# The product that picks the tokens of the second expert pair, moved ahead of the first pair's gate and up products

## The chip, the cores and the metric

The kernel runs on one NeuronCore of a Trainium2 chip. The metric is the device time of one execution in microseconds (us). Three executions of the kernel before took 1514.11, 1519.95 and 1521.13 us; their median is 1519.95 us. A fourth execution was recorded by the hardware profiler and took 1516.05 us. All rows shown here come from that one. In the profile, PE is TensorE (the matrix engine), PEld its weight loads, DVE is VectorE, ACT is ScalarE, POOL is GpSimd and SP is SyncE, the engine that issues the large DMAs. An issue on a queue of an engine is written SPq, ACTq or POOLq.

## The reference

One step of a hybrid decoder with one layer: 256 prompt tokens and 8 sample tokens, width 2048. After the attention part (stick-breaking and forgetting heads, a paged cache, an output projection, a residual add) comes a mixture of 32 experts, of which each token uses two. The part that matters here is this, cut from the reference:

```python
u = rms_norm(h, norm_ffn_g)                       # 264 tokens x 2048
lg = u @ w_rg + b_rg                              # choice of 1 of 4 groups
le = einsum('td,gde->tge', u, w_re) + b_re        # choice of 2 of 8 experts in it
comb = one_hot(chosen experts) * gate             # 264 x 32
h = silu(u @ w_gate[e]) * (u @ w_up[e])           # per expert e, 2048 -> 256
f = sum_e (h * comb[:, e]) @ w_down[e]            # 256 -> 2048
y = rms_norm(h_residual + f, norm_final_g)
```

Everything is float32. The weights of an expert are three matrices of 2 MB each, so the 32 experts are 96 loads of 2048 KB.

## The kernel before, in words

The kernel computes expert by expert, two experts (a pair, k = 0 and 1) at a time, in 16 pairs numbered n. A pair has 128 slots for tokens, 64 for each expert; the first 8 slots of each expert hold the 8 sample tokens, the others prompt tokens that were routed to it. There may be further pairs for experts that overflow; they are guarded by a run-time test.

Each pair needs these steps, and the engines take them in a fixed order that the program text sets:

- **tokens(n)** on PE (L1901): 32 matrix products of 128x128 with a 0/1 selection `pick_tok`, made by POOL, that pick the prompt tokens of pair n out of `qo` and leave them transposed in banks 4 to 7 of the accumulator memory. ACT copies the four banks to `xgT` (`tokens` on ACT, L2012), but not before the gate and up products of the pair before have read the old `xgT` (semaphore gu1).
- **gate_up(k, n)** on PE (L1912 and L1914): gate and up product of expert k. It waits for its two weights in the buffer `ws`, slots 3k and 3k+1.
- **turn_over(k, n)** on PE (L1921): two transposes of the result, after DVE has copied it to `gu`.
- **silu** on ACT (L2020) and a multiplication on DVE (L2120) give `hT`.
- **down(k, n)** on PE (L1934): the down product, with the weight in slot 3k+2; it waits for `hT`. In all pairs with a following pair the whole of `xgT` for that next pair has to be written first: `pe.wait_ge(E["xgT"], 4 * n + 8)` stands ahead of down(0, n), since down writes banks 4 to 7.
- POOL scatters the result rows to memory (`y_rows`).

The order on PE in a pair is gate_up(0), gate_up(1), turn_over(0), tokens(n+1), turn_over(1), down(0), down(1). On ACT it is silu(0), tokens(n+1), silu(1), and a copy of half the down result.

Pair 0 is special. Its tokens were picked at the end of the attention part (L1148). The sample tokens are finished only here: PE sums their rows in `sample_rows` (L1941, 32 products with 8 columns as the profile counts them) between the two gate_up, DVE normalises them, PE computes their router logits in `sample_logits` (L1949) behind gate_up(1), and DVE runs `sample_route`, a chain of some 25 small operations that ends in `s_r` (L2094, semaphore sr2). ACT waits for sr2, computes one exponential (L2045), and only then enters its own pair 0: silu(0), tokens(1), silu(1). On PE, turn_over(1, 0) waits for slc 3, the two additions that take the logits out of bank 3.

SP loads the weights. There are six slots, one for each weight of a pair, so a load of pair n+1 can only be issued once the product of pair n that reads the slot has finished. The order of issue is slots 0, 1 (waiting for gate_up(0)), 3, 4 (gate_up(1)), 2 (down(0)), 5 (down(1)), see L170. The six weights of pair 0 are issued earlier, as the output projection frees the slots.

Of the kernel before, what the change touches and what calls it, by code (L numbers as in the profile page):

```python
# [75 lines left out]
def wait_past(eng, sem, value):  # L76

    if not isinstance(value, int) or value > 0:
        eng.wait_ge(sem, value)
# [642 lines left out]
def token_cols(qo, t, c):  # L722

    return qo[:, 8 * t + c // 2, c % 2 * P:(c % 2 + 1) * P]
# [1025 lines left out]
def experts(nc, ctx, ws, W, a, ident, ones, iota, gcol, lastq, xT, xn, qo, xgT, in_slot, in_pair, pick_tmp, pick_tok, wr, br, bank, sem, E, dest, gates, extra,  # L1750
# [48 lines left out]
    with nc.Block() as block:  # L1799
# [91 lines left out]
        def _(pe):  # L1891
            def tokens(n, stored, i):


                pe.wait_ge(E["xg"], n + 1)
                wait_past(pe, E["yc0"], 2 * stored)
                wait_past(pe, E["yc1"], 2 * stored)
                for k in range(4):
                    for c in range(4):
                        for t in range(2):  # L1900
                            mm = pe.matmul(bank[4 + k][:, c * P:(c + 1) * P], token_cols(qo, t, 4 * k + c), pick_tok[:, i, t, :],  # L1901
                                           start=(t == 0), stop=(t == 1))
                    mm.then_inc(E["xgp"], 1)

            def gate_up(k, n):

                wg, wu = 3 * k, 3 * k + 1
                pe.wait_ge(W[wg], 16 * (n + FIRST[wg]))
                pe.wait_ge(W[wu], 16 * (n + FIRST[wu]))
                for c in range(KC):  # L1910
                    lhs = xgT[:, c, k * SLOTS:(k + 1) * SLOTS]
                    pe.matmul(bank[2 * k][0:SLOTS, 0:256], lhs, ws[:, wg, c * 256:(c + 1) * 256],  # L1912
                              start=(c == 0), stop=(c == KC - 1))
                    mm = pe.matmul(bank[2 * k][SLOTS:P, 0:256], lhs, ws[:, wu, c * 256:(c + 1) * 256],  # L1914
                                   start=(c == 0), stop=(c == KC - 1))
                mm.then_inc(E[f"gu{k}"], 1)

            def turn_over(k, n):
                pe.wait_ge(E[f"guc{k}"], n + 1)
                for j in range(2):  # L1920
                    mm = pe.transpose(bank[2 * k + 1][:, j * P:(j + 1) * P], gu[k][:, :].rearrange("s (p j) -> s j p", j=2)[:, j, :],  # L1921
                                  ident[:, :])
                mm.then_inc(E[f"t{k}"], 1)

            def down(k, n):

                wd = 3 * k + 2
                pe.wait_ge(W[wd], 16 * (n + FIRST[wd]))
                pe.wait_ge(E[f"h{k}"], n + 1)
                for dc in range(2):  # L1930
                    for j in range(2):
                        for q in range(4):
                            h0, d0 = q // 2 * HALF, j * D + q % 2 * 1024 + dc * 512
                            mm = pe.matmul(bank[4 + 2 * k + dc][q * HALF:(q + 1) * HALF, :], hT[k][:, j, h0:h0 + HALF],  # L1934
                                           ws[:, wd, d0:d0 + 512], start=(j == 0), stop=(j == 1))
                mm.then_inc(E[f"y{k}"], 1)

            def sample_rows():
                part = xn[:, :, :].rearrange("p c t -> p (c t)")
                for c in range(KC):  # L1940
                    mm = pe.matmul(bank[3][:, c * NB:(c + 1) * NB], part[:, c * P:(c + 1) * P], lastq[:, 0:NB], start=True, stop=True)  # L1941
                mm.then_inc(E["sf"], 1)

            def sample_logits():

                pe.wait_ge(E["sun"], 1)
                for c in range(KC):
                    for r0 in (0, HALF):
                        mm = pe.matmul(bank[3][r0:r0 + NB, P:P + NG + NE], xn[:, c, SEQ:T], wr[:, c, 0:NG + NE],  # L1949
                                       start=(c == 0), stop=(c == KC - 1))  # L1950
                mm.then_inc(E["sl"], 1)

            def sample_rest():

                pe.wait_ge(E["yc0"], 2 * EXP_PAIRS - 2)
                pe.wait_ge(E["dst"], 1)
                pe.wait_ge(F["sel"], 1)
                pe.transpose(bank[4][:, 0:P], x_s[:, :, :].rearrange("p n c -> p (n c)"), ident[:, :])
                pe.matmul(bank[4][:, P:P + 2], spread[:, :], gates[0:NB, 2, :], start=True, stop=True).then_inc(F["hs"], 1)

            def pair(n, ahead, first=False, last=False, i=0):
                pe.wait_ge(E["xgT"], 4 * n + 4)
                gate_up(0, n)
                if last:
                    sample_rest()
                if first:
                    sample_rows()
                gate_up(1, n)
                if first:
                    sample_logits()  # L1970
                turn_over(0, n)
                if ahead:
                    tokens(n + 1, n, i)
                if first:
                    pe.wait_ge(E["slc"], 3)
                turn_over(1, n)
                if ahead:
                    pe.wait_ge(E["xgT"], 4 * n + 8)
                if last:
                    pe.wait_ge(F["hsc"], 2)  # L1980
                down(0, n)
                down(1, n)

            pair(0, True, True, i=1)
            with pe.Fori(0, EXP_PAIRS // 2 - 1) as m:
                for i in range(2):
                    pair(2 * m + 1 + i, True, i=i)
            pair(EXP_PAIRS - 1, False, last=True)
            with pe.If(in_use(pe, 0) > 0):
                for n in range(EXP_PAIRS, PAIRS):  # L1990
# [219 lines left out]
```

## Time and profile before

| what | value |
|---|---|
| median of three runs | 1519.95 us |
| profiled execution | 1516.05 us |
| span of its instructions | 1514.3 us |
| PE busy, of the span | 1315.7 us (87%) |
| DVE busy | 673.4 us (44%) |
| ACT busy | 233.6 us (15%) |
| read from memory over the span | 558.26 MB, 379 GB/s with the writes |

The 1.75 us between the span and the time of the execution lie outside the first and last instruction. Busy shares are averages over the attention part (to about 991 us) and the expert part (from there on), which have different limits; the stage that the change touches has to be read by itself. A stretch is given as "from:to" in us from the start of the span. The DMA share of a stretch is the mean busy share of the 16 DMA engines, and it can read slightly above 1. PEclk is the clock granted to TensorE, where 1.00 is 2.4 GHz and 0.50 is 1.2 GHz.

### The profile page before, as it was taken

To read this page: it belongs to the slowest core of one execution; us is meant where nothing else is said; L and a number is where in the kernel's file an instruction comes from. 1 tells how busy PE (TensorE), PEld (TensorE's weight loads), DVE (VectorE), ACT (ScalarE), POOL (GpSimd) and SP (SyncE) were. 2 spreads that over 40 slices of the span, in tenths; PEclk is the share of its full clock that TensorE was granted. 3 is DMA by queue.
4 is the path that set the end of the run, shared out by engine and by line. 5 is a ranking of instruction groups with operands and counts; after the bars stand their busy time and mean duration, and the time that the engine had idled before them with its cause. 6 is when DMAs were issued, how large, how long until landed. Compare 5 with 4: busy or idle time off the path is not lost. (4 is left out here: it accounts for less than half of the span.)

```text
span 1514.3 us, 26133 instructions
## 1 busy us (share of the span) xinstructions
PE 1315.7 (87%) x8622; PEld 870.3 (57%) x8622; DVE 673.4 (44%) x4778; ACT 233.6 (15%) x453; POOL 75.4 (5%) x119
## 2 busy tenths in 40 slices
PE   7999788889789899856899987789999999999992
PEld 4678455566556566533667743466666565655561
DVE  4437855676676675677846466021000100000004
ACT  2111002112212212213011021101111010111011
POOL 1000000000000000001000001001100010001000
PEclk8899989899999999976999998979999999999997
DMA  9776999999999999999999989999999999999984
GB/s 302 248 260 229 385 397 391 396 383 381 382 377 390 383 379 392 387 405 398 351 403 402 401 320 390 399 414 379 422 428 428 427 424 423 422 419 414 416 341 178
DMA packets 170382, 570.39 MB, mean 377 GB/s; under 512 B 17401, under 2 KB 75562, under 8 KB 156954
## 3 DMA queue, kind: packets, MB, share of 16 engines
q1 hardware_dynamic: 145616, 541.70, 91.4%
q10 hardware_dynamic: 21762, 22.58, 4.3%
q0 software_dynamic: 2896, 4.86, 0.9%
q8 instruction: 45, 0.74, 0.2%
q14 instruction: 63, 0.52, 0.1%
HBM read 558.26 MB, written 15.67 MB: 379 GB/s over the span
## 5 line engine op out<-in xcount | busy, mean ns | idle before, releaser
L128 DVE CUSTOM_DVE_ANT_0 ws<-ws,xgT 128x128 f32<-128x128 f32 x1792 | 387.8, 284 | 204.7 <-DMA ws<-in_cache_fox_k 186.0
L979 PE MATMUL bank<-xn,ws 128*128 128x264 f32 x1152 | 289.9, 407 | 10.5 <-DMA ws<-in_w_in 10.5
L979 PEld LDWEIGHTS bank<-xn,ws 128*128 128x128 f32 x1152 | 223.0, 199 | 110.9 <-issue 54.8
L1912 PE MATMUL bank<-ws,xgT 128*64 128x256 f32 x1024 | 231.4, 386 | 16.7 <-DMA ws<-in_w_expert_up 12.1
L1914 PE MATMUL bank<-ws,xgT 128*64 128x256 f32 x1024 | 231.5, 386 | 0.0
L964 PE MATMUL bank<-ws,PR 128*32 128x512 f32 x1024 | 150.8, 668 | 78.3 <-DMA ws<-in_cache_fox_v 73.8
L1912 PEld LDWEIGHTS bank<-ws,xgT 128*64 128x64 f32 x1024 | 140.3, 139 | 104.6 <-issue 22.2
L128 DVE DVE_READ_ACCUMULATOR2_ANT Z<- 128x1 f32 x1792 | 141.8, 79 | 0.0
L1914 PEld LDWEIGHTS bank<-ws,xgT 128*64 128x64 f32 x1024 | 140.3, 139 | 0.0
L2113 DVE COPY gu<-bank 128x256 f32<-128x256 f32 x32 | 13.6, 425 | 269.4 <-PE bank L1914 269.4
L1084 PE MATMUL bank<-qo,ws 128*128 128x256 f32 x512 | 117.0, 387 | 6.2 <-DVE qo L1521 5.2
L1934 PE MATMUL bank<-ws,hT 128*32 128x512 f32 x1024 | 113.2, 594 | 7.1 <-ACT xgT L2012 6.9
L1084 PEld LDWEIGHTS bank<-qo,ws 128*128 128x128 f32 x512 | 97.7, 193 | 31.5 <-issue 16.6
L1901 PE MATMUL bank<-xg,qo 128*128 128x128 f32 x960 | 109.7, 275 | 0.0
L1901 PEld LDWEIGHTS bank<-xg,qo 128*128 128x128 f32 x960 | 108.5, 192 | 0.0
L964 PEld LDWEIGHTS bank<-ws,PR 128*32 128x32 f32 x1024 | 21.5, 112 | 119.8 <-DMA ws<-in_cache_fox_v 91.8
L523 PE MATMUL bank<-xn,ws 128*128 128x264 f32 x384 | 86.8, 387 | 0.0
L523 PEld LDWEIGHTS bank<-xn,ws 128*128 128x128 f32 x384 | 72.6, 190 | 14.1 <-issue 2.0
L1934 PEld LDWEIGHTS bank<-ws,hT 128*32 128x32 f32 x1024 | 32.0, 110 | 76.7 <-issue 67.0
L607 DVE CUSTOM_DVE_ANT_0 ws<-ws,xgT 128x128 f32<-128x128 f32 x256 | 55.3, 287 | 39.5 <-DMA ws<-in_cache_sb_k 15.6
L2120 DVE TENSOR_TENSOR hT<-si,bank 128x128 f32<-128x128 f32 x32 | 9.2, 288 | 108.3 <-ACT si L2020 108.2
L1848 POOL DMA_INDIRECT y_rows<-ys,dest x32 | 29.5, 922 | 403.6 <-DVE ys L2124 338.6
(433 smaller groups left out, 971.4 us busy)
## 6 DMA issues: line engine op xcount, KB each, us to landing
ws<-in_cache_sb_k SPq DMA_DIRECT2D x128, 512.0 KB, 9.1
ws<-in_cache_fox_k SPq DMA_DIRECT2D x128, 512.0 KB, 13.0
ws<-in_cache_sb_v SPq DMA_DIRECT2D x128, 512.0 KB, 9.2
ws<-in_cache_fox_v SPq DMA_DIRECT2D x128, 512.0 KB, 12.8
ws<-in_w_expert_gate SPq DMA_DIRECT2D x32, 2048.0 KB, 16.1
ws<-in_w_expert_up SPq DMA_DIRECT2D x32, 2048.0 KB, 20.0
ws<-in_w_expert_down SPq DMA_DIRECT2D x32, 2048.0 KB, 16.9
ws<-in_w_in SPq DMA_DIRECT2D x24, 2048.0 KB, 21.3
```

The costliest lines, as they stand in the source:

```text
L128: ins = dve.tensor_tensor_reduce(k, k, qb[:, (g * H + h) * HD:(g * H + h + 1) * HD], 1.0, 0.0, ALU.mult, ALU.add, Z[:, n % 2, g, h, t:t + 1])
L523: mm = pe.matmul(bank[4 + k % 4][:, 0:T], chunk(n)[:, c, m * P:(m + 1) * P], xn[:, c, :], start=(c == 0), stop=(c == KC - 1))
L607: ins = dve.tensor_tensor_reduce(k, k, qb[:, (g * H + h) * HD:(g * H + h + 1) * HD], 1.0, 0.0, ALU.mult, ALU.add, Z[:, 0, g, h, t:t + 1])
L964: mm = pe.matmul(bank[0][r0:r0 + 32, :], PR[:, g, t, :], vring[:, u, g, half * 512:(half + 1) * 512], start=(t == 0), stop=(t == PAGES - 1))
L979: mm = pe.matmul(out[:, 0:T], w[:, c, m * P:(m + 1) * P], xn[:, c, :], start=(c == 0), stop=(c == KC - 1))
L1084: mm = pe.matmul(out, ws[:, 4 + r, k0:k0 + P], qo[:, 8 * r + c, 0:SEQ], start=(r == 0 and c == 0 and m % 2 == 0), stop=(r == 1 and c == 7) ...
L1848: pool.indirect_dma_start(y_half, bass.IndirectOffsetOnAxis(ap=dest[0:rows, 2 * n + k:2 * n + k + 1], axis=0), ys[k][0:rows, :], None, bou ...
L1901: mm = pe.matmul(bank[4 + k][:, c * P:(c + 1) * P], token_cols(qo, t, 4 * k + c), pick_tok[:, i, t, :], start=(t == 0), stop=(t == 1))
L1912: pe.matmul(bank[2 * k][0:SLOTS, 0:256], lhs, ws[:, wg, c * 256:(c + 1) * 256], start=(c == 0), stop=(c == KC - 1))
L1914: mm = pe.matmul(bank[2 * k][SLOTS:P, 0:256], lhs, ws[:, wu, c * 256:(c + 1) * 256], start=(c == 0), stop=(c == KC - 1))
L1934: mm = pe.matmul(bank[4 + 2 * k + dc][q * HALF:(q + 1) * HALF, :], hT[k][:, j, h0:h0 + HALF], ws[:, wd, d0:d0 + 512], start=(j == 0), stop ...
L2113: dve.tensor_copy(gu[k][:, :], bank[2 * k][:, 0:256]).then_inc(E[f"guc{k}"], 1)
```

## The change

For pair 0 alone, the call of tokens(1) is taken from its place between turn_over(0, 0) and turn_over(1, 0) and put ahead of gate_up(0, 0). The other pairs keep their order. Nothing is added or taken away, and no other engine's program is changed: ACT still copies the picked tokens behind silu(0), and not before gu1.

```diff
             def pair(n, ahead, first=False, last=False, i=0):
                 pe.wait_ge(E["xgT"], 4 * n + 4)
+                if first:
+                    tokens(n + 1, n, i)
                 gate_up(0, n)
                 if last:
                     sample_rest()
@@
                 if first:
                     sample_logits()
                 turn_over(0, n)
-                if ahead:
+                if ahead and not first:
                     tokens(n + 1, n, i)
                 if first:
                     pe.wait_ge(E["slc"], 3)
```

The first place is on PE at the start of the expert part. L1746 and L1890 are branches at the block's entry, L1901 is tokens, L1912 and L1914 are the gate and the up product. A row "x32" is 32 instructions of the program in a row.

```order
 L1746 UNCONDITIONAL_BRANCH
 L1890 UNCONDITIONAL_BRANCH
+L1901 MATMUL bank<-xg,qo 128x128 x32
 L1912 MATMUL bank<-ws,xgT 64x256
 L1914 MATMUL bank<-ws,xgT 64x256
```

The 32 products of tokens(1) now stand ahead of the first gate product.

The second place is on PE behind gate_up(1, 0). L1949 is sample_logits, L1921 the transposes of turn_over, L1934 the down products.

```order
 L1914 MATMUL bank<-ws,xgT 64x256
 L1949 MATMUL bank<-wr,xn 8x36 x32
-L1921 MATMUL bank<-ident,gu 128x128 x2
-L1901 MATMUL bank<-xg,qo 128x128 x32
-L1921 MATMUL bank<-ident,gu 128x128 x2
+L1921 MATMUL bank<-ident,gu 128x128 x4
 L1934 MATMUL bank<-ws,hT 32x512 x32
```

Nothing but the four transposes is left between the logits and the down products.

## Rows read from the trace of the kernel before

**Rows 1.** Page, part 4: the chain that ended last, by line.
```profile
DMA ws<-in_w_expert_up 14%; PE bank L1912 11%; PE bank L1934 3%; PE bank L1901 2%; PE bank L1914 0%; DVE ws L2138 0%; DMA ws<-y_rows 0%; ACT xgT L2012 0%; SPq L170 0%; PE bank L1941 0%; DVE ws L2155 0%; DMA y_rows<-ys,dest 0%; DVE ws L2144 
```

**Rows 2.** Stretches: PE, PEld, DVE, ACT, POOL busy, PEclk, DMA share, GB/s.
```profile
1028.00:1030.00 2.00, 2.00 (x24) 0.64 (x20) 0.05 (x1) 0.00 (x0) 0.00 (x0) 1.00 0.12 41
1030.00:1032.00 2.00, 2.00 (x24) 0.65 (x20) 1.24 (x2) 0.00 (x0) 0.00 (x0) 1.00 0.62 123
...
1032.00:1466.00 434.00, 416.35 (x3723) 268.03 (x3711) 38.44 (x85) 53.35 (x116) 51.05 (x56) 1.00 1.00 421
```

**Rows 3.** Issues on SP's queue in order of time: start, us, what.
```profile
980.68 0.33 SPq L170 DMA_DIRECT2D ws<-in_w_expert_down  x1
1003.81 0.34 SPq L170 DMA_DIRECT2D ws<-in_w_expert_gate  x1
...
1016.22 0.33 SPq L170 DMA_DIRECT2D ws<-in_w_expert_gate  x1
...
1029.94 3.77 SPq L170 DMA_DIRECT2D ws<-in_w_expert_down  x2
```

**Rows 4.** DMAs issued in 980:981, then in 1016:1016.5: size, us to landing.
```profile
ws<-in_w_expert_down SPq DMA_DIRECT2D x1, 2048.0 KB, 28.7
...
ws<-in_w_expert_gate SPq DMA_DIRECT2D x1, 2048.0 KB, 8.9
```

**Rows 5.** PE in order of time, pair 0: start, us, what [idle before <-releaser].
```profile
994.97 0.66 PE L1912 MATMUL bank<-ws,xgT 128*64 128x256 f32 x1 [4.65 <-PEq L85]
...
1003.55 3.74 PE L1941 MATMUL bank<-lastq,xn 128*128 128x8 f32 x32
...
1015.96 1.21 PE L1949 MATMUL bank<-wr,xn 128*8 128x36 f32 x64
...
1017.45 7.31 PE L1901 MATMUL bank<-xg,qo 128*128 128x128 f32 x64
1024.59 0.40 PE L1921 MATMUL bank<-ident,gu 128*128 128x128 f32 x2
1026.24 7.07 PE L1934 MATMUL bank<-ws,hT 128*32 128x512 f32 x64 [1.25 <-ACT xgT L2012]
```

**Rows 6.** DVE and ACT in order of time, behind the sample logits.
```profile
1017.30 0.40 DVE L2090 TENSOR_TENSOR s_lg<-bank,br 8x36 f32<-8x36 f32 x2 [0.76 <-PE bank L1949]
...
1022.46 0.15 DVE L2094 TENSOR_TENSOR s_r<-s_top 40x1 f32<-40x1 f32 x1
...
1022.87 1.28 ACT L2020 ACT_TABLE_LOAD   x1
...
1024.34 1.85 ACT L2012 ACTIVATE xgT<-bank 128x448 f32<-128x448 f32 x4
```

**Rows 7.** The chain in order of time: start, us, what.
```profile
1084.76 7.08 PE bank L1934 x64
...
1114.01 7.07 PE bank L1934 x64
...
1381.48 22.97 DMA ws<-in_w_expert_up
...
1412.22 23.02 DMA ws<-in_w_expert_up
```

**Rows 8.** Stretches around slow clocks, columns as in rows 2.
```profile
990.50:994.90 4.40, 0.00 (x0) 0.00 (x0) 0.88 (x4) 0.21 (x1) 0.00 (x0) 0.50 0.99 421
...
996.00:998.00 2.00, 2.00 (x13) 1.18 (x11) 0.00 (x0) 0.00 (x0) 0.19 (x1) 0.50 0.97 401
998.00:1000.00 2.00, 2.00 (x21) 1.47 (x19) 0.00 (x0) 0.94 (x1) 1.15 (x5) 0.98 1.02 430
...
1008.00:1010.00 2.00, 2.00 (x14) 1.16 (x12) 0.54 (x2) 0.00 (x0) 0.00 (x0) 0.58 0.95 364
1010.00:1012.00 2.00, 2.00 (x14) 1.12 (x12) 0.00 (x0) 0.00 (x0) 0.00 (x0) 0.56 1.10 462
```

**Rows 9.** PE's waits in 1165:1470: us in total, times, longest.
```profile
PE bank L1912 <- DMA ws<-in_w_expert_up: 12.1, 9, 2.1
```

## The prediction

> **What bounds the kernel now.** I read the chain of waits first, then the busy times by stretch, then SP's queue, then PE, ACT and DVE in order of time. The chain [rows 1] shows the expert part as a mixture: a weight transfer (14% of the span) and PE products (L1912 11%, L1934 3%, L1901 2%). In order of time it changes sides. Until some 1164 us it runs on PE alone, with 29.25 us from one pair's down products to the next's (1114.01 - 1084.76) [rows 7]. At the end it runs through the transfers, 30.74 us per pair (1412.22 - 1381.48) [rows 7], and PE waits for weights 9 times, 12.1 us in all [rows 9].
>
> That invites a wrong reading: PE seems to have 12 us to spare, so a delay of PE in pair 0 would be swallowed. The stretches say otherwise [rows 2]. From 1032 to 1466 us the DMA engines are busy for a share of 1.00, at 421 GB/s. The work left for them there is fixed: the two down weights of pair 1 and six weights for each of pairs 2 to 15, 86 loads of 2.097 MB, 180.4 MB; 434 us at 421 GB/s are 182.7 MB, the rest being result rows. So this queue can't catch up. The last gap in it lies just before, 1028 to 1032 us, with shares of 0.12 and 0.62 [rows 2]. It ends because SP issues the down weights of pair 1 at 1029.94 [rows 3], when down(0, 0) has read slot 2. What moves that issue moves the end of the kernel by the same amount. That is the quantity to compute.
>
> **What the change does, step by step.**
>
> *Start.* PE's first gate product starts at 994.97, released by PE's own sequencer at the block's entry (PEq L85), not by a weight or by tokens [rows 5]. tokens(1) will start there too. It does not start earlier, so none of the 4.65 us of idleness ahead of it is used. Its inputs are ready: POOL is to make the selection for pair 1 before the block, and its later ones have their place behind the sample routing. No weight wait hides it: gate_up ran at 994.97 without one.
>
> *Added ahead of gate_up(0).* 32 products, which are 64 records, take 7.14 us at the full clock from the start of the first to that of the transpose behind them (1024.59 - 1017.45) [rows 5]. I take 7.2. Before, PE's clock was at 0.50 (1.2 GHz) until 998 and at 1.00 (2.4 GHz) after [rows 8]. This slow stretch now falls on tokens(1) instead of gate_up(0). As both are dense rows of products, 3 us of either cost the same 1.5 us, so this adds nothing. gate_up(0) ends 7.2 us later, at about 1010.7; so do sample_rows, gate_up(1) and the logits, whose end moves from 1017.17 to about 1024.4.
>
> *Removed behind the logits.* Here 7.31 us of products go [rows 5], but they did not set the start of down(0). What did is the routing: L1949 ends at 1017.17, DVE adds at 1017.30 and reaches s_r at 1022.46, ACT then has its exponential, loads a table (1.28 us from 1022.87), does silu and copies xgT from 1024.34 for 1.85 us, and down(0) starts at 1026.24 on that last copy [rows 5, 6]. From the logits' end to down(0) that makes 9.07 us, none of them tokens(1). tokens(1) lay wholly in this shadow: turn_over(1) was over 1.25 us before down(0) started. The chain of 9.07 us stays, since no instruction of DVE or ACT is moved. So the stall does not go. PE's idleness there grows from 1.25 to about 9.07 - 2 x 0.40 (both turn_over) = 8.3 us, and the removed products bring 0. Could ACT's copies begin earlier, now that the banks are full early? No: ACT has them behind silu(0), and silu(0) behind the exponential. Gain 0.
>
> *The new idleness and the clock.* Twice in this stage the clock is at its lower level: through the 4.65 us of idleness from 990.3 on and until 998.1 [rows 5, 8], and from about 1008.3 to 1011.8, following sample_rows, 3.74 us of products with only 8 columns [rows 5]. The times are worked out from shares of 0.58 and 0.56 in two stretches of 2 us: (1 - 0.58) / 0.5 x 2 and (1 - 0.56) / 0.5 x 2 make 1.7 and 1.8 us [rows 8]. An idleness of 8.3 us is longer than the one at 990, so I expect down(0) to start at 1.2 GHz. With a slow stretch as long as that from 994.97 to 998, 3.1 us, half of it is lost: 1.6 us. Ends: 0 if the clock doesn't fall, and 3.5 us if all of down(0), half of the 7.07 us of rows 5, runs at half speed. I take 1.6, the row nearest in kind. The other slow stretch, behind sample_rows, costs half of its 3.5 us, 1.8; it should come again. It may be missed (-1.8) or last twice as long (+1.8); I take 0.
>
> The trace shows the clock low through and after PE's idleness of 4.65 us, and high 3.1 us after work resumed. The Trainium skill, "TensorE: Matmul & The Clock Gate", section "The HAM clock gate (the 'warmup' mystery)", says likewise that idleness throttles the engine to half rate and sustained work releases it; this rule speaks against a change that gathers PE's idleness in one place. By it the sum is 8.8 us; without any fall it is 7.2.
>
> *DMA.* Slots 0 and 1 are freed at about 1011.0 instead of 1003.81 [rows 3]. The last weight of pair 0 was issued at 980.68 and landed 28.7 us later, at 1009.4 [rows 3, 4]: the queue will run dry here for 2 to 3 us. Slots 3 and 4 are issued at about 1023.4 instead of 1016.22 [rows 3]; the two loads before them need 4.2 MB / 0.421, 10 us, and end at about 1022.5: a second gap of 1 to 2 us. With 8.9 us to the landing of the first of a set [rows 4] and 5 more for the second, that batch has landed by about 1037. The down weight is issued at 1029.94 + 7.2 + 1.6 = 1038.7. So the queue is dry before it, as before, nothing is carried over, and the issue moves by the whole 8.8 us. POOL's selection for pair 2 waits for the routing and moves along.
>
> *Later pairs* keep their order and find all of it shifted together. The period of 29.25 us is shorter than the queue's 30.74, so any further PE lag of a few us (the clock staying low into down(1)) is absorbed by the queue; the 8.8 us are not, because they stood empty in the queue itself.
>
> **Sum.** tokens(1) ahead 7.2, tokens(1) behind 0, slow clock at down(0) 1.6, second slow stretch 0: 8.8 us, 0.58%. Against the profiled execution, 1516.05 + 8.8 = 1524.9. The median of three runs is 3.9 us above that execution, and the four times known reach from 1514.11 to 1521.13. I place the changed kernel's median on the mean of the profiled time and the median, 1518.0, which makes 1526.8, rounded to 1527.
>
> **The rivals.**
>
> *A, forecast, 0.50.* +8.8, own range +7.2 to +10.5: 1525.2 to 1528.5 from 1518.0, and 1523 to 1531 with 2 us of the runs' spread on either side.
>
> *B, only the products count, or less, 0.20.* The clock doesn't fall in the new idleness, or the slow stretch behind sample_rows is missed: +7.2 - 1.8 = +5.4 up to +7.2, 1523.4 to 1525.2. For it: in another run the slow stretches may lie elsewhere, and one profile can't tell how firmly they are tied to the work. Against it: 8.3 us is long beside 4.65.
>
> *C, the clock stays low, 0.13.* All of down(0) at half speed, or a longer slow stretch behind sample_rows: 7.2 + 3.5 = 10.7 up to 12.5, 1528.7 to 1530.5. For it: the clock was low for all of 990.5 to 994.9 and 3.1 us more [rows 8], and a new slow stretch may begin late in the idleness. Against: from 994.97 on dense work brought the full clock back within 3.1 us.
>
> *D, not slower: the delay is swallowed, 0.17.* This is the reading by the 12.1 us of rows 9: what ends the kernel is the pace of the transfers after 1164 us, and if the queue could run faster than it did in 1032:1466, the 29.25 us pace of PE would be overtaken later and the lost us come back. It decides from a rate of 182.7 MB in 434 - 8.8 us, 430 GB/s instead of 421, 2% more. Then the result is 1516.05, or 1518 on the mean. For it: a single stretch of 2 us shows 462 GB/s [rows 8]. Against it: a share of 1.00 over 434 us leaves nothing to take up. A small part of this case, with a missed slow stretch and a quick run, would even read as faster.
>
> **How the numbers follow.** About 0.5% (7.6 us) is what a measurement of this kernel tells from no change. Case A lies above it for some 0.43 of its 0.50, C with all of its 0.13, and 0.02 come from B by scatter: slower 0.58. Same: 0.07 of A, 0.18 of B, 0.12 of D, 0.37. Faster: 0.05 of D. The range 1520 to 1532 takes A, nearly all of B and C, and the upper end of D; A's own is 1523 to 1531.
>
> **What would show it.** L1901 x64 ahead of the first L1912, starting at about 995. The first gate weight of pair 1 issued near 1011, the second near 1023.4, the first down weight near 1038 to 1039. PE idle for about 8 us before the first L1934, released by ACT's xgT copy, with 9.07 us from the end of L1949 to it. A clock of 0.50 in the first half of down(0). DMA shares well below 1 near 1010 and for 3 to 5 us before 1039, and 1.00 from there to about 1475. I am wrong if down(0) starts less than 6 us later than 1026.24, or if the last weights land at their old time although it starts later.

## The result, and the profile after

The changed kernel took 1528.12 us, the median of 14 executions (1521.58 to 1530.14). The kernel before, run beside it, took 1517.65 us (1514.11 to 1521.13, 14 executions). The ratio is 1.0067 with a 95% interval of 1.0053 to 1.0080: slower by 10.2 us, between 8.0 and 12.1. The forecast was +8.8 and 1527.

The chain of waits of the changed kernel is almost that of [rows 1] (the page's part 4; in the program text the lines behind the edit are two higher, so L2014 is the old L2012). L1901 went from 2% to 3%:

```profile
DMA ws<-in_w_expert_up 14%; PE bank L1912 10%; PE bank L1934 3%; PE bank L1901 3%; PE bank L1914 0%; DMA ws<-y_rows 0%; DVE ws L2140 0%; PE bank L1941 0%; ACT xgT L2014 0%; SPq L170 0%; DVE ws L2157 0%; DMA y_rows<-ys,dest 0%; DVE ws L2146 
```

Shares don't say where the time came from. PE in order of time does. The rows answer to [rows 5], and come from an execution of 1530.08 us:

```profile
996.05 10.16 PE L1901 MATMUL bank<-xg,qo 128*128 128x128 f32 x64 [4.65 <-PEq L85]
...
1013.21 4.89 PE L1941 MATMUL bank<-lastq,xn 128*128 128x8 f32 x32
...
1027.21 1.21 PE L1949 MATMUL bank<-wr,xn 128*8 128x36 f32 x64
1028.36 1.16 PE L1921 MATMUL bank<-ident,gu 128*128 128x128 f32 x4
1037.50 9.71 PE L1934 MATMUL bank<-ws,hT 128*32 128x512 f32 x64 [7.98 <-ACT xgT L2014]
```

The picking products stand first. Behind the logits PE sits idle for 7.98 us where it had 1.25, and the releaser is the same, ACT's copy of xgT. From the end of the logits (1028.42) to the down products are 9.08 us; before they were 9.07. ACT in that time, as in [rows 6]:

```profile
1034.13 1.28 ACT L2022 ACT_TABLE_LOAD   x1
1035.42 0.28 ACT L2022 ACTIVATE si<-bank 128x128 f32<-128x128 f32 x1
1035.60 1.85 ACT L2014 ACTIVATE xgT<-bank 128x448 f32<-128x448 f32 x4
```

The down products then take 9.71 us instead of 7.07. SP's queue, to be held against [rows 3]:

```profile
1013.48 0.34 SPq L170 DMA_DIRECT2D ws<-in_w_expert_gate  x1
...
1027.47 0.33 SPq L170 DMA_DIRECT2D ws<-in_w_expert_gate  x1
...
1043.84 3.77 SPq L170 DMA_DIRECT2D ws<-in_w_expert_down  x2
```

The last issue moved by 13.90 us, and the span grew by 14.0 (1514.3 to 1528.3). Of this, 1.08 us lie ahead of the block: its first product starts at 996.05 instead of 994.97. The stretches (columns as in rows 2) show the queue dry three times, and full from then on; the last row answers to 1032:1466:

```profile
1010.00:1012.00 2.00, 2.00 (x22) 1.31 (x20) 0.00 (x0) 0.00 (x0) 0.00 (x0) 1.00 0.04 12
1026.00:1028.00 2.00, 2.00 (x61) 1.35 (x59) 0.46 (x2) 0.00 (x0) 0.00 (x0) 1.00 0.00 0
...
1040.00:1042.00 2.00, 2.00 (x16) 0.59 (x12) 0.00 (x0) 0.00 (x0) 0.00 (x0) 0.50 0.00 0
...
1046.00:1480.00 434.00, 416.41 (x3721) 268.24 (x3715) 38.43 (x85) 53.33 (x116) 50.92 (x56) 1.00 1.00 422
```

Two executions of one kernel differ by some us in the clock alone, as before_again shows below, so the 13.9 us between these two traces must not be taken for the effect. For that I split the way from the first PE product of the block, S, to the issue of the first down weight of pair 1, D. The granted clock of a stretch gives what the lower level cost in it: half of the time at 0.50, which is (1 - clock) x length. The clock is given to 0.01, so over 33 us this is good to some 0.2 us. The changed kernel's two stretches, with PE's long idleness between them left out since a slow clock costs nothing there:

```profile
996.05:1029.52 33.47, 33.31 (x292) 26.38 (x292) 2.87 (x12) 1.28 (x1) 1.33 (x5) 0.81 0.76 302
1037.50:1043.84 6.34, 6.34 (x36) 1.63 (x40) 0.29 (x1) 0.12 (x1) 0.59 (x1) 0.58 0.22 93
```

33.47 x 0.19 = 6.4 and 6.34 x 0.42 = 2.7, together 9.0 us lost. S to D is 47.79 us; at the full clock it would be 38.8. For the kernel before the same working gives 34.97 and, with

```profile
994.97:1024.99 30.02, 30.02 (x292) 23.38 (x292) 8.49 (x45) 3.60 (x6) 1.35 (x6) 0.89 1.00 411
```

a loss of 3.3, so 31.7 us. The change costs 7.1 us at equal clocks. Together with the 2.7 us at the down products and the 3.1 us by which the loss ahead of them grew (6.4 against 3.3), that is, but for rounding, the 12.8 us by which S to D grew.

### The profile page after: what moved, and what is told of

It is laid out like the page before. It is cut to its first block and busy times, and to the rows that moved or that the text cites. A ratio compares the mean times of both kernels' runs of the same rounds, so it can differ in the third digit from the quotient of the medians.

```text
span 1528.3 us, 26134 instructions
## 1 busy us (share of the span) xinstructions
PE 1329.6 (87%) x8622; PEld 880.2 (58%) x8622; DVE 673.8 (44%) x4778; ACT 233.5 (15%) x453; POOL 73.1 (5%) x119
## 5 line engine op out<-in xcount | busy, mean ns | idle before, releaser
L1912 PE MATMUL bank<-ws,xgT 128*64 128x256 f32 x1024 | 230.4, 385 | 12.0 <-DMA ws<-in_w_expert_up 12.0
L1914 PE MATMUL bank<-ws,xgT 128*64 128x256 f32 x1024 | 230.4, 385 | 0.0
L1912 PEld LDWEIGHTS bank<-ws,xgT 128*64 128x64 f32 x1024 | 139.8, 139 | 99.8 <-issue 16.8
L1914 PEld LDWEIGHTS bank<-ws,xgT 128*64 128x64 f32 x1024 | 139.8, 139 | 0.0
L1934 PE MATMUL bank<-ws,hT 128*32 128x512 f32 x1024 | 115.8, 605 | 13.8 <-ACT xgT L2014 13.6
L1901 PE MATMUL bank<-xg,qo 128*128 128x128 f32 x960 | 112.5, 279 | 4.7 <-PEq L85 4.7
L1901 PEld LDWEIGHTS bank<-xg,qo 128*128 128x128 f32 x960 | 111.3, 196 | 4.7 <-issue 4.7
L1934 PEld LDWEIGHTS bank<-ws,hT 128*32 128x32 f32 x1024 | 32.4, 111 | 85.7 <-issue 69.2
L1848 POOL DMA_INDIRECT y_rows<-ys,dest x32 | 29.4, 920 | 406.2 <-DVE ys L2126 338.6
```

The lines of the kernel that those rows point to most:

```text
L1848: pool.indirect_dma_start(y_half, bass.IndirectOffsetOnAxis(ap=dest[0:rows, 2 * n + k:2 * n + k + 1], axis=0), ys[k][0:rows, :], None, bou ...
```

## The experiments

The time given for a kernel is the median of 6 to 12 executions, against the kernel before timed beside it; the two repeats are single executions. The table is read from one trace of each kernel and gives S to D, the loss to the clock worked out as above, the difference of the two, and the span behind D.

| kernel | S to D | lost to clock | at full clock | D | span | span - D |
|---|---|---|---|---|---|---|
| before | 34.97 | 3.3 | 31.7 | 1029.94 | 1514.3 | 484.4 |
| before_again | 37.85 | 6.3 | 31.6 | 1033.21 | 1517.2 | 484.0 |
| e3_before_few | 37.87 | 6.3 | 31.6 | 1032.20 | 1516.4 | 484.2 |
| e6_route_early | 35.46 | 4.7 | 30.8 | 1031.17 | 1517.3 | 486.1 |
| after | 47.79 | 9.0 | 38.8 | 1043.84 | 1528.3 | 484.5 |
| after_again | 47.78 | 9.0 | 38.8 | 1042.46 | 1527.1 | 484.6 |
| e4_after_few | 37.84 | 5.1 | 32.7 | 1031.76 | 1516.3 | 484.5 |
| e1_middle | 43.88 | 5.1 | 38.8 | 1036.64 | 1521.1 | 484.5 |
| e5_fill | 45.18 | 6.5 | 38.7 | 1042.69 | 1526.8 | 484.1 |
| e7_tokens_in_route | 36.61 | 3.5 | 33.1 | 1029.54 | 1518.6 | 489.1 |
| e2_route_early | 38.61 | 6.5 | 32.1 | 1033.83 | 1523.8 | 490.0 |

**The products left out, at the new place (e4_after_few).** In `tokens` of pair 0 alone 4 of the 32 products stay. The kernel thus leaves out most of the tokens of pair 1, and its result for them is not that of the reference; no wait and no other instruction is missing.

```diff
-                    tokens(n + 1, n, i)
+                    few_tokens(n + 1, n, i)     # one product for each of the 4 banks
                 gate_up(0, n)
```

> The changed kernel with 4 instead of 32 products in tokens(1) of pair 0; 28 products, and with them the correct tokens of pair 1, are left out. Theory: what is left of the change is 0.9 us of products at full clock; down(0, 0) starts 1 to 4 us later than in the kernel before, the rest being PE's clock in the idleness of 8 us that stays; the time is +1 to +4 us. Rival (the place of the wait or the order of the queue costs, not the products): +8 to +10 us as with all of them.

Measured: 1518.24 us, ratio 1.0003 (0.9991 to 1.0015), +0.5 us. That lies a little under the theory's +1 to +4 and far from the rival's +8 to +10. The idleness of 8 us is still there, and the down products are slow, which costs 2.3 us up to D. The median doesn't show these, and in the trace they are made up for by the clock elsewhere: it did not fall around sample_rows, so the whole loss is 5.1 us, between the 3.3 and 6.3 of the kernel before.

```profile
993.92 2.04 PE L1896 MATMUL bank<-xg,qo 128*128 128x128 f32 x8 [4.65 <-PEq L85]
...
1025.80 9.32 PE L1941 MATMUL bank<-ws,hT 128*32 128x512 f32 x64 [7.99 <-ACT xgT L2021]
```

So it is the products, not the place of their wait. At the full clock D comes 1.0 us later than before (32.7 against 31.7), about the length of the four products left.

**The products left out, at the old place (e3_before_few).** The same four in the kernel before, with the same tokens left out.

```diff
-                    tokens(n + 1, n, i)
+                    (few_tokens if first else tokens)(n + 1, n, i)
```

> The kernel before with 4 instead of 32 products in tokens(1) of pair 0, at their old place; 28 products, and with them the correct tokens of pair 1, are left out. Theory (there the products lie wholly in the shadow of the routing): down(0, 0) still starts 9.07 us after the end of the logits, and the time is that of the kernel before, -1 to +3 us, above it only where the clock falls in PE's new idleness of 7 us. Rival (7 us of products cost 7 us at either place): -6 to -7 us.

Measured: 1518.36 us, ratio 1.0013 (0.9994 to 1.0031), +2.0 us, within the theory's -1 to +3. Nothing gained, where the rival wanted 6 to 7 us:

```profile
1015.28 1.21 PE L1956 MATMUL bank<-wr,xn 128*8 128x36 f32 x64
1016.42 0.51 PE L1928 MATMUL bank<-ident,gu 128*128 128x128 f32 x2
1016.77 1.06 PE L1896 MATMUL bank<-xg,qo 128*128 128x128 f32 x8
1017.66 0.40 PE L1928 MATMUL bank<-ident,gu 128*128 128x128 f32 x2
1025.56 10.00 PE L1941 MATMUL bank<-ws,hT 128*32 128x512 f32 x64 [7.50 <-ACT xgT L2019]
```

The products became idleness, 7.50 us instead of 1.25, and the down products start 9.07 us behind the logits (1025.56 - 1016.49), to the hundredth as in [rows 5]. The clock falls here too, in the old order, and costs 3.0 us at the down products. At the full clock D is where it was, 31.6. With e4 this shows both halves: the same products are free behind the logits and cost their length ahead of them.

**Half way (e1_middle).**

```diff
-                if first:
-                    tokens(n + 1, n, i)
                 gate_up(0, n)
+                if first:
+                    tokens(n + 1, n, i)
```

> tokens(1) of pair 0 stands between gate_up(0) and sample_rows, ahead of the logits still, but behind the products that free slots 0 and 1. Theory (the 32 products delay the logits, and the routing chain of 9 us behind the logits holds down(0, 0)): the first issue for pair 1 stays about 8.8 us behind the first PE product of the block, as in the kernel before, but the first down weight is again issued 7 to 13 us later than there, and the time is +7 to +11 us over the kernel before. Rival (the loss is that slots 0 and 1 are freed late, so that the queue runs dry at 1011 us): most of the loss goes, 0 to +4 us.

Measured: 1526.88 us, ratio 1.0064 (1.0043 to 1.0084), +9.7 us, as the theory had it. The trace is of the fastest of its six executions, 1522.88 us. Slots 0 and 1 are freed at their old time, 9.28 us behind S (before 8.84), and the loss is all there: at the full clock D is as late as in the changed kernel, 38.8.

```profile
1002.04 0.34 SPq L170 DMA_DIRECT2D ws<-in_w_expert_gate  x1
...
1036.64 3.77 SPq L170 DMA_DIRECT2D ws<-in_w_expert_down  x2
```

The idleness ahead of the down products is that of the changed kernel, but the clock was low for a shorter part of them, and 1.4 us are lost there instead of 2.7:

```profile
1031.62 8.38 PE L1934 MATMUL bank<-ws,hT 128*32 128x512 f32 x64 [7.99 <-ACT xgT L2014]
```

**The idleness filled (e5_fill).**

```diff
                 turn_over(1, n)
+                if first:
+                    for _ in range(32):
+                        pe.matmul(bank[0][:, 256:384], ident[:, :], ones[:, :], start=True, stop=True)
                 if ahead:
                     pe.wait_ge(E["xgT"], 4 * n + 8)
```

> The changed kernel with 32 products of 128x128 into an unused part of bank 0 put behind turn_over(1, 0), where PE is idle for 8 us before the first down. They add no result. Theory (the clock falls in this idleness and down(0) runs at half speed for 2.6 us of loss): down(0) and down(1) together take near 7.1 us again instead of 9.7, and the time is 1.5 to 3 us below that of the changed kernel, +6 to +9 over the kernel before. Rival (the clock's state there is not tied to the idleness): the same +10 us, down at 9 us or more.

Measured: 1524.69 us, ratio 1.0039 (1.0023 to 1.0056), +5.9 us, at the lower end of the +6 to +9 expected. That is 3.4 us less than the changed kernel's median, and 4.3 us less by the two ratios, where 1.5 to 3 were expected.

```profile
1030.83 7.31 PE L1981 MATMUL bank<-ones,ident 128*128 128x128 f32 x64
1038.99 7.08 PE L1934 MATMUL bank<-ws,hT 128*32 128x512 f32 x64 [0.85 <-ACT xgT L2017]
```

With PE at work until 0.85 us ahead of them the down products run at the full clock, 7.08 us instead of 9.71. The clock's part at this place is shown, and hangs on the idleness; the start of the down products itself is still set by ACT's copy. The two intervals against the kernel before overlap by a hair at 1.0053 to 1.0056, so the size of the gain is better taken from the traces: 2.6 us from S to D (47.79 - 45.18). The trace is of one of its slower executions, 1528.59 us, whose S comes at 997.51.

**The routing moved (e2_route_early).** tokens(1) stays early; the logits come early too.

```diff
                 if first:
+                    sample_rows()
                     tokens(n + 1, n, i)
                 gate_up(0, n)
                 if last:
                     sample_rest()
                 if first:
-                    sample_rows()
-                gate_up(1, n)
-                if first:
                     sample_logits()
+                gate_up(1, n)
                 turn_over(0, n)
...
+                if first:
+                    sample_norm()
                 for k in range(2):
                     dve.wait_ge(E[f"gu{k}"], n + 1)
...
-                    if first:
-                        (sample_norm, sample_route)[k]()
+                    if first and k == 0:
+                        sample_route()
```

> tokens(1) stays ahead of gate_up(0) as in the changed kernel, but sample_rows stands at the block's start and the logits ahead of gate_up(1), with DVE's normalisation and routing moved to match; the routing then runs beside gate_up(1). Theory (the loss is that tokens(1) left the shadow of the routing chain): PE's idleness ahead of the first down falls from 8.0 to about 2.7 us, down(0, 0) starts some 0.9 us later than in the kernel before at equal clocks, and the time is 0 to +4 us over the kernel before. Rival (any 7 us of products ahead of gate_up(0) cost their length, for the weights of pair 1 come late): still +8 to +11 us.

Measured: 1524.68 us, ratio 1.0043 (1.0029 to 1.0057), +6.5 us. Between the theory and the rival: a miss. The part on PE came somewhat better than expected. The idleness went down to 0.83 and 0.80 us, 1.6 together instead of 2.7, and D at the full clock is 32.1, 0.4 behind the kernel before instead of 0.9:

```profile
1027.51 0.51 PE L1921 MATMUL bank<-ident,gu 128*128 128x128 f32 x2
1028.85 0.48 PE L1921 MATMUL bank<-ident,gu 128*128 128x128 f32 x2 [0.83 <-DVE gu L2116]
1030.13 7.07 PE L1934 MATMUL bank<-ws,hT 128*32 128x512 f32 x64 [0.80 <-ACT xgT L2013]
```

But the span behind D is 490.0 us, not 484.4. D did not end the last dry spell here, and the theory had counted with D alone. SP's queue:

```profile
1019.58 0.34 SPq L170 DMA_DIRECT2D ws<-in_w_expert_gate  x1
1020.02 0.38 SPq L170 DMA_DIRECT2D ws<-in_w_expert_up  x1
1027.77 0.33 SPq L170 DMA_DIRECT2D ws<-in_w_expert_gate  x1
```

The queue was dry from about 1010 until this issue at 1019.58, as a stretch with columns as in rows 2 shows:

```profile
1010.00:1018.00 8.00, 8.00 (x75) 6.00 (x76) 0.00 (x0) 0.00 (x0) 0.00 (x0) 1.00 0.01 2
```

It was never dry again: when D came at 1033.83, the four loads before it (19.9 us from 1019.58 on) had not all landed. What counts is the issue that ends the *last* dry spell. A load of 2.097 MB at 421 GB/s [rows 2] lasts 4.98 us; four loads more than from D make 19.9, and 1019.58 + 19.9 + 484.4 = 1523.9. The span is 1523.8.

**A test of that (e7_tokens_in_route).** tokens(1) in the shadow of a routing that begins early, ahead of gate_up(1).

```diff
                 gate_up(0, n)
...
                 if first:
                     sample_rows()
+                    turn_over(0, n)
+                    sample_logits()
+                    tokens(n + 1, n, i)
                 gate_up(1, n)
-                if first:
-                    sample_logits()
-                turn_over(0, n)
-                if ahead:
+                if not first:
+                    turn_over(0, n)
+                if ahead and not first:
                     tokens(n + 1, n, i)
```

(The edit is against the kernel before; on DVE the normalisation and the routing both follow the first copy.)

> Pair 0 in the order gate_up(0), sample_rows, turn_over(0), logits, tokens(1), gate_up(1), turn_over(1), down; DVE's normalisation and routing stand behind its first copy. The routing now runs beside tokens(1) and gate_up(1), slots 0 and 1 are freed at their old time, and only slots 3 and 4 some 8 us later. Theory 1 (the time hangs on the start of the first down alone): the first down weight is issued 34 to 36 us behind the first PE product of the block, as in the kernel before with 34.97, so the time is that of the kernel before, -1 to +1 us. Theory 2, formed after e2_route_early (the time is the issue that ends the queue's last dry spell, plus 4.98 us for each load still to come, plus what follows): the queue runs dry between the landing of slots 0 and 1, near 27 us behind the first product, and the issue of slot 3 near 29.4 us behind it; from there 88 loads are to come, which gives +3 to +6 us over the kernel before, though the first down starts no later.

Measured: 1523.18 us, ratio 1.0043 (1.0023 to 1.0063), +6.5 us. Theory 1, -1 to +1, is out. Theory 2 had +3 to +6; +6.5 is just above it, and its interval, 3.5 to 9.6, reaches into it. D comes 36.61 us behind S, a little over the 34 to 36 expected, yet at 1029.54 no later than in [rows 3], and the span is 4.3 us longer. The queue:

```profile
1024.07 0.33 SPq L170 DMA_DIRECT2D ws<-in_w_expert_gate  x1
1024.50 0.38 SPq L170 DMA_DIRECT2D ws<-in_w_expert_up  x1
1029.54 3.77 SPq L170 DMA_DIRECT2D ws<-in_w_expert_down  x2
```

and the stretch ahead of it, PE at work and no transfer:

```profile
1018.00:1024.00 6.00, 5.88 (x56) 3.62 (x52) 0.07 (x1) 0.07 (x1) 0.55 (x1) 1.00 0.00 0
```

1024.07, two loads more (10.0), and 484.4 make 1518.5; the span is 1518.6. The issue itself came 31.1 us behind S, where the expectation had 29.4.

**The kernel before with early routing (e6_route_early).** The moves of e2_route_early, with those on DVE, but without tokens(1) in front.

```diff
+                if first:
+                    sample_rows()
                 gate_up(0, n)
                 if last:
                     sample_rest()
                 if first:
-                    sample_rows()
-                gate_up(1, n)
-                if first:
                     sample_logits()
+                gate_up(1, n)
                 turn_over(0, n)
```

> The kernel before, tokens(1) at its old place, with sample_rows at the block's start and the logits ahead of gate_up(1), DVE's work moved to match. Theory: the routing is done before tokens(1) ends, PE's idleness ahead of down(0, 0) falls from 1.25 to about 0.6 us; at equal clocks -0.7 us, together with the clock -3 to +2 us. Rival (the routing chain of 9 us was a bound by itself before): -5 us or more.

Measured: 1517.44 us, ratio 1.0003 (0.9986 to 1.0019). No gain, as the theory had it (-3 to +2). PE's last idleness fell to 0.40 us, and D at the full clock is 0.9 us earlier (30.8). But sample_rows at the block's start ran at the low clock and delayed the first issue of pair 1 to 15.5 us behind S, so that the queue ran dry there:

```profile
995.71 6.96 PE L1941 MATMUL bank<-lastq,xn 128*128 128x8 f32 x32 [4.50 <-PEq L85]
...
1019.52 7.31 PE L1901 MATMUL bank<-xg,qo 128*128 128x128 f32 x64
...
1027.46 7.07 PE L1934 MATMUL bank<-ws,hT 128*32 128x512 f32 x64 [0.40 <-ACT xgT L2012]
```

The rule of the last dry spell gives 1011.25 + 19.9 + 484.4 = 1515.6 here, and the span is 1517.3. The 1.7 us are not explained.

**Second traces (before_again, after_again).**

> The kernel before, once more, for a second trace: its slow stretches of the clock in 980 to 1030 us. If these are tied to the work, they lie where they lay (to 998 and 1008.3 to 1011.8); if not, they lie elsewhere and the first down weight is issued up to 3 us earlier or later behind the first product of the block than 34.97 us.

> The changed kernel, once more, for a second trace. Its executions reach from 1521.6 to 1530.1 us. If the clock makes this spread, the trace shows other lengths for the slow stretches in tokens(1), behind sample_rows and in down(0), and the time differs by half of the difference in their sum.

before_again took 1518.93 us. Its slow stretches lie at the same two places and are longer: behind S the clock is low for 5.8 us instead of 3.2, and around sample_rows, which take 4.58 us instead of 3.74, for 6.8 instead of 3.4. They put D 37.85 us behind S, 2.9 more than before, the whole of it clock (6.3 against 3.3 lost).

```profile
1005.22 4.58 PE L1941 MATMUL bank<-lastq,xn 128*128 128x8 f32 x32
...
1029.51 7.07 PE L1934 MATMUL bank<-ws,hT 128*32 128x512 f32 x64 [1.25 <-ACT xgT L2012]
```

after_again took 1528.89 us and repeats the first trace, so it does not show what made the fast executions of 1521.6 to 1524.8:

```profile
994.68 10.16 PE L1901 MATMUL bank<-xg,qo 128*128 128x128 f32 x64 [4.65 <-PEq L85]
...
1036.12 9.70 PE L1934 MATMUL bank<-ws,hT 128*32 128x512 f32 x64 [7.99 <-ACT xgT L2014]
```

## Why the prediction was right, point by point

*tokens(1) ahead of gate_up(0), 7.2 us.* Right. At the full clock S to D grew by 7.1 us in both traces of the changed kernel, and e4 takes this away with the products.

*tokens(1) behind the logits, 0.* Right, and shown by e3: leaving 28 of the products out there did not change the 9.07 us, and the time did not fall.

*The idleness grows to 8.3 us.* 7.98: the four transposes take 1.1 us instead of 0.8, with a wait for DVE's additions among them.

*The clock at down(0), 1.6 us.* Right in kind, too small: 6.34 x 0.42 = 2.7 us in both traces of the changed kernel. I had taken the slow stretch from S on, 3.1 us, as the measure; at down(0) the clock was low for 5.3 of the 6.34 us to D. Neither length is firm. Behind S it was 3.1 or 3.2 us in two traces, before and e3_before_few, and 5.8 to 6.0 in five others; the loss at down(0) was 1.4, 2.3 and 3.0 us in e1, e4 and e3. e5 removes it by removing the idleness. The rule of the Trainium skill that the prediction cited ("TensorE: Matmul & The Clock Gate", section "The HAM clock gate (the 'warmup' mystery)": idleness throttles to half rate, sustained work releases) holds at this place: 7.98 us of idleness, then 9.71 us for down; 0.85 us, then 7.08.

The row that I had compared it with, the idleness of 4.65 us at 990.3, doesn't bear the comparison. The clock had been low since 984.4, some 6 us before this idleness, while PE was busy with products of 8 columns:

```profile
981.33 7.10 PE L1170 MATMUL bank<-lastq,xn 128*128 128x8 f32 x32 [0.70 <-ACT xn L1346]
...
984.50:985.00 0.50, 0.50 (x4) 0.50 (x4) 0.00 (x0) 0.00 (x0) 0.00 (x0) 0.50 1.16 492
```

That an idleness makes the clock fall is shown by the experiments, not by that row.

*The other slow stretches, 0 net.* Open. Between the first traces they cost 3.1 us more (6.4 against 3.3), but before_again has 6.3 with the old program, so the old order can have it too. How often is not known: in the old order the traces have 3.3, 6.3 and 3.3 (before, before_again, e3_before_few), in the order of the changed kernel 6.4, 6.4 and 6.5 (after, after_again, e5_fill). These few traces can't tell whether the change makes the longer stretches more frequent.

*The sum.* 7.1 + 2.7 = 9.8 us at D, against 10.2 (8.0 to 12.1) measured and 8.8 forecast. What the forecast lacks against 9.8 is the clock at down(0). That 9.8 lies so near to 10.2 is in part luck: if the other slow stretches cost the changed kernel 1 or 2 us more on average, the sum is 11 to 12, which the interval holds as well.

*DMA.* The three dry spells came ahead of the three issues for which they were forecast, each 2.5 to 5.1 us later than forecast with PE, and the 434 us of full queue moved as a block. Rival D, that the delay is swallowed, is out: the rate there was 422 GB/s against 421, where it would have needed 430. The prediction took D because its issue ends the last gap of the queue, and that condition held here. It is a condition, which my expectation of e2 forgot: e2 and e7 show kernels where an earlier issue ends the last dry spell, and D alone gives a time that is 5.6 and 4.7 us too short.

No version here beats the kernel before. That the 7.1 us are the length of the products, and that their old place was free, is shown by e3, e4 and e1. What sets the lengths of the slow stretches stays open.

## What to carry to other kernels

Work that lies in the shadow of a chain on other engines is free there and costs its full length ahead of that chain's start, as long as the chain sets the end; before moving it, find what releases the instruction behind it. Where a transfer queue is full from some point to the end, look for the issue that ends its last dry spell: here the time was that issue plus the loads still to come, to within 0.4 us in ten of the eleven traces, and the 12 us for which PE waits for weights later on [rows 9] gave nothing back. Gathering an engine's idleness in one place can cost a second time, in the clock.

## What the runs showed of the hardware

TensorE's clock fell to 1.2 GHz in every idleness of 7.5 to 8 us behind the logits, and the 64 records of down products after it took 8.38 to 10.00 us instead of 7.07, in all five traces with such an idleness; in the other six, with 0.40 to 1.25 us, they took 7.07 or 7.08. It also fell during or just behind the 32 records of sample_rows with 8 columns, though these kept the engine busy: in two traces of the kernel before the clock was low there for 3.4 and 6.8 us, and in e4_after_few not at all. At the end of the attention part it fell 3 us into 7.1 us of such products (L1170). Through such differences, at this place and behind S, two executions of one program lie 2.9 us apart at D, against a spread of 1514.1 to 1521.1 us in its times.
